# Accumulating DMAs with their addend read from main memory in two halves, and an own program for the first FFN body

## The chip, the cores and the metric

One core of one Trainium2 chip runs the whole kernel. The metric is the device time of one execution in microseconds. TensorE (PE) does the matmuls; ScalarE (ACT), VectorE (DVE) and GpSimd (POOL) prepare operands; SyncE (SP) issues loads. POOL issues the accumulating DMAs. Each engine runs its own instruction list in order, and the lists are tied together by semaphores.

## The reference, cut to what matters

```python
DEPTH, SEQ, D_MODEL = 2, 256, 2048
D_FF = -(-8 * D_MODEL // (3 * 256)) * 256          # 5632
def swiglu(h, w_gate, w_up, w_down):
    return (jax.nn.silu(h @ w_gate) * (h @ w_up)) @ w_down
...
        x = x + rms_norm(m.astype(x.dtype), norm_mix_post[layer])
        h = rms_norm(x, norm_ffn_pre[layer])
        f = swiglu(h, ffn_w_gate[layer], ffn_w_up[layer], ffn_w_down[layer])
        x = x + rms_norm(f.astype(x.dtype), norm_ffn_post[layer])
```

Two layers: the first has a recurrence and a windowed attention as its mixer, the second a differential attention. All is float32. The change touches the FFN (swiglu) of both layers and the last matmuls of the block before it.

## The kernel before, in words

**Split operands.** Every float32 matmul is made of three passes over float32r operands: high part times high part, high times low part of the weight, low part of the activation times high part of the weight. So each 1 MB weight block (128 partitions x 4 x 512) is loaded into a `raw` buffer by SP, ACT copies it to `w_hi` (`hi`, L1035, four buffers), and DVE subtracts to get `w_lo` (`lo`, L1724, three buffers). `lo` of unit u waits until unit u-3 has left PE, `hi` until unit u-4 has.

**The FFN.** The 5632 hidden columns are taken in 11 blocks of 512. The first block is computed in the mixer's style ("head": alternating gate and up units for four row blocks; its last two units are put together by `head_end`, L340). The ten others are computed in ten *bodies*. In body j, PE multiplies the gate and up weights of block j+1 and, beside it, the down projection of block j. Gate and up products are made by a seven-product scheme (P1 to P7, each for the row pairs A and B, 14 units of 12 matmuls); the down projection has four units of 24 matmuls (d0, d1, d3, d2). With eight transposes of the hidden block (`turn`) that makes 18 entries per body. `ENTRIES` gives their order on PE, and the function `block` in each engine's program writes the order out by hand for ACT (L1313), PE (L1669) and DVE (L2079).

**Sums of weights.** P5, P6, P4 and P7 need sums of weight blocks. Four of them (P5A, P6A, P6B, P4B, the `FORMS`) are added in place by DVE (`form`, L1731). The other four (P5B, P7A, P7B, P4A, the `TRANSFERS`) are added in place by an accumulating DMA that POOL issues (`transfer`, L2243): destination `raw[total]`, source `raw[part]`, both on chip, 128 pieces of 8 KB. Before it issues, POOL waits until the total's own `lo` is done and the addend has landed; for P7B also until P5B has landed. ACT's `hi` of that entry waits for the DMA.

**Sums of activations ("lefts").** The scheme also needs sums S1 to S4 of activation blocks for both halves A and B. They are computed once per layer: DVE adds (`left_total`, L1747, 0.7 us each), ACT makes the high part (`left_high`, L1256), DVE the low part (`left_low`, L1787). Before the change S1A, S3A, S2A and S4A are totalled in `head_end`; the low parts of S1A, S2A and S4A too; the rest is made inside the first body, between its entries, under `if body.first`.

**Where the hidden block enters.** `down` (L1637) needs the hidden block transposed: PE's `turn`, ACT's `block_high` (L1251) for `y_hi`, and DVE's `block_low` for `y_lo`. In ACT's `block`, `high(body, "P5A")` stands before `block_high`; in DVE's, `form(P5A)`, `low(d0)`, the four `left_total`s of B (first body only) and `low(P5A)` stand before `block_low`. On PE, d0 follows P1A directly.

**Buffers.** In the FFN eight 1 MB buffers hold weights: three `raw` ones and, by reuse, `gx`, `queries`, `gq` and the two halves of `xs`. `gq` holds the gains of the norm until the block before the head is done (`POST_GAIN`), and `xs` holds the residual, which SP spills to main memory at the end of the head (`spill`). `place_loads` (L580) plans which buffer each load takes, and what it waits for: a buffer is free when the last `lo`, `form` or transfer that reads it is done. `EARLY` loads (d0, g2, u2) are issued ahead of the first body; `released` lists the readers.

Of the kernel before, what the change touches and what calls it, by code (L numbers as in the profile page):

```python
# [27 lines left out]
ALU = mybir.AluOpType  # L28
# [58 lines left out]
class Slot:  # L87


    def __init__(self, u, kg, n, first, last, w, cb=0, region="h", layer=0):  # L90
# [15 lines left out]
FORMS_AHEAD = FORMS[:0]  # L106
# [25 lines left out]
class Body:  # L132


    def __init__(self, layer, j, index, u, e, m, n_head):

        self.layer, self.j, self.index, self.first = layer, j, index, j == 0
        self.base, self.e, self.m = u, e, m
        self.u = {name: u + i for i, name in enumerate(ENTRIES)}
        self.head_gate, self.head_up, self.next, self.prev = n_head, n_head + 1, None, None  # L140
        self.form = {name: len(FORMS) * index + i + 1 for i, name in enumerate(FORMS)}
# [16 lines left out]
def loads_of(body):  # L158

    return tuple(name for name in LOADS if not (body.first and name in EARLY))  # L160

# [20 lines left out]
class Plan:  # L182
# [3 lines left out]
    def __init__(self):  # L186
# [7 lines left out]
        self.place, self.after, self.heads_of, self.head_units, self.x_read, self.wholes, self.last_body = {}, {}, [], [], [], {}, []  # L194

# [144 lines left out]
def head_end(slots, body):  # L340
# [14 lines left out]
    tasks = half(gate, 0) + [Task("early_load", src=body, what=EARLY[2])] + [total(name) for name in TOTALS[:3]]  # L355
    tasks += high_ahead(gate.u - 1, gate) + low_ahead(gate.u - 1, gate) + [left(name) for name in HEAD_LEFT[0]]
    tasks += half(gate, 1) + gate.post + half(up, 0) + [total(TOTALS[3]), Task("spill", 2 * body.layer + 1, slot=up)]
    tasks += high_ahead(gate.u, up) + half(up, 1) + up.post + low_ahead(gate.u, up)
    tasks += [Task("form", src=body, what=name) for name in FORMS_AHEAD] + [left(name) for name in HEAD_LEFT[1]]
# [36 lines left out]
def boundary(b, before, after):  # L396
# [19 lines left out]
    tasks += [hi(u + 11), lo(u + 10), turn(3, 1), lo(u + 11), square(0, 0), hi(u + 12)] + half(a4, 1)  # L416
# [98 lines left out]
def make_plan():  # L515
    plan, before = Plan(), None
    for layer in range(2):
# [14 lines left out]
        plan.head_units.append([slot.u for slot in head])  # L532
        plan.bodies += NF - 1
# [46 lines left out]
def place_loads(plan):  # L580
# [9 lines left out]
    def released(body, name):  # L590
# [7 lines left out]
        def added(entry):  # L598
            if entry in TRANSFERS:
                return entry, 16 * (body.index + 1), body.u[entry] - 1  # L600
            return "form", body.form[entry], body.u[entry] - 1
        if name[0] == "g":
            return (read("P2" + pair), added("P4" + pair)) if second else (read("P4" + pair),)
        return (read("P3" + pair), added("P6" + pair), added("P7" + pair)) if second else (read("P7" + pair),)

    for part in plan.parts:
        for task in part.tasks or ():
            if task.kind == "early_load":
                take((task.src.index, task.what), (RAW + EARLY.index(task.what),), released(task.src, task.what))
            elif task.kind == "tile_unit" or task.kind == "half" and task.t == 0 and task.passes[0] == 0:  # L610
                take(task.slot.u, range(RAW), (("lo", task.slot.u + 1, task.slot.u),))
# [12 lines left out]
def trunk(nc, x, norm_mix_pre, norm_mix_post, norm_ffn_pre, norm_ffn_post,  # L624
# [9 lines left out]
    with ExitStack() as ctx:  # L634
# [198 lines left out]
        def transfer_done(eng, body, name):  # L833

            eng.wait_ge(transferred[name], 16 * (body.index + 1))
# [24 lines left out]
        def _(sp):  # L860
# [5 lines left out]
            def wait_free(waits):  # L866

                for what, value in waits:
# [4 lines left out]
                    elif what in TRANSFERS:  # L873
                        sp.wait_ge(transferred[what], value)
# [79 lines left out]
            def load_slot(slot):  # L954
# [5 lines left out]
                else:  # L960
                    load(slot.u, src)

            def task_of(task):
                if task.kind == "tile_unit" or task.kind == "half" and task.t == 0 and task.passes[0] == 0:
                    load_slot(task.slot)
                elif task.kind == "early_load":
                    if task.what == EARLY[0]:
                        sp.wait_ge(s_done, plan.heads_of[task.src.layer])
                    elif task.what == EARLY[2]:
                        counts = plan.y_counts[2 * task.src.layer + 1]  # L970
                        sp.wait_ge(yg_pool, counts["pool"])
                        sp.wait_ge(yg_dve, counts["dve"])
# [40 lines left out]
        def _(act):  # L1013
# [299 lines left out]
            def block(body):  # L1313
# [8 lines left out]
                if not body.first:  # L1322
                    unload(body.prev, 2, 0)
                seed(body, 0, 1)
                if not body.first:
                    unload(body.prev, 2, 1)
# [6 lines left out]
                if body.first:  # L1333
                    left_high("S1B", body.layer)
# [6 lines left out]
                if body.first:  # L1341
                    left_high("S2B", body.layer)
# [4 lines left out]
                if body.first:  # L1347
                    left_high("S4B", body.layer)
                high(body, "P3B")
                if body.first:  # L1350
                    left_high("S3A", body.layer)
                    left_high("S3B", body.layer)
# [23 lines left out]

            act.dma_start(pre[:, :, :], pre_T).then_inc(pre_in, 16)
# [3 lines left out]
            for part in plan.parts:  # L1381
# [4 lines left out]
                for body in part.bodies:  # L1386
# [8 lines left out]
        def _(pe):  # L1395
# [189 lines left out]
            for part in plan.parts:  # L1585
# [106 lines left out]
                for body in part.bodies:  # L1692
# [6 lines left out]
        def _(dve):  # L1699
# [379 lines left out]
            def block(body):  # L2079
# [4 lines left out]
                if not body.first:  # L2084
                    gated(body.prev, 0)
                if not body.first:
                    gated(body.prev, 1)
                form(body, "P5A")
                low(body, "d0")
                if body.first:  # L2090
                    for name in TOTALS[4:]:
                        left_total(name, body.layer)
# [5 lines left out]
                if body.first:  # L2098
                    left_low("S1B", body.layer)
# [3 lines left out]
                if body.first:  # L2103
                    left_low("S2B", body.layer)
                low(body, "P6B")
                form(body, "P4B")
                if body.first:
                    left_low("S4B", body.layer)
                low(body, "P3B")
                if body.first:  # L2110
                    left_low("S3A", body.layer)
# [196 lines left out]
```

## Time and profile before

| | us |
|---|---|
| median of 3 runs (lowest, highest) | 2176.39 (2174.54, 2178.85) |
| profiled execution, whole | 2174.88 |
| its span, first to last instruction | 2173.1 |
| PE busy | 2145.7 (99%) |
| DVE, ACT, POOL busy | 1700.2, 1490.0, 228.7 |

Each number of a stretch is read from the profiled execution, whose time is 1.5 us under the median. The layers' FFN bodies lie at 423 to 1030 us and at 1525 to 2130 us.

### The profile page before, as it was taken

The numbers are of one execution on the slowest core, as the hardware profiler recorded it, in microseconds if no ns is written. First come the engines' busy times: TensorE is split into PE (matmuls) and PEld (weight loads), VectorE is DVE, ScalarE is ACT, GpSimd is POOL, SyncE is SP. The second block draws the span as 40 slices with busy tenths as digits, with TensorE's granted clock in tenths as the row PEclk, the third lists the DMA queues.
The fourth block names the chain that finished last, engine by engine and source line by source line (L and its number), as shares of the span: only waits on it lengthen the run. The fifth ranks groups of instructions, "written<-read, shape, count | busy, mean of one in ns | idle before, by whom it ended". The sixth has DMA issues, their size and how long they took to land.

```text
span 2173.1 us, 26552 instructions
## 1 busy us (share of the span) xinstructions
PE 2145.7 (99%) x9771; PEld 1767.7 (81%) x9771; DVE 1700.2 (78%) x1538; ACT 1490.0 (69%) x1774; POOL 228.7 (11%) x274
## 2 busy tenths in 40 slices
PE   9999999999999999999999999999999999999998
PEld 7888888778888888888887787788788888888886
DVE  5577467898988888888755656677998888888886
ACT  6677544777777777777655555547677777777774
POOL 0851000000000000000021001001000000000001
PEclk9999999999999999999999999999999999999999
DMA  9545446789999999998564454557899999999984
GB/s 310 190 154 191 155 137 211 242 261 277 264 265 263 302 288 279 282 288 240 177 213 143 150 171 138 187 171 245 244 281 267 303 284 279 284 287 266 266 258 155
DMA packets 226559, 508.82 MB, mean 234 GB/s; under 512 B 13736, under 2 KB 16384, under 8 KB 214656
## 3 DMA queue, kind: packets, MB, share of 16 engines
q1 hardware_dynamic: 214192, 422.68, 55.1%
q0 software_dynamic: 11520, 83.89, 19.5%
q8 instruction: 79, 1.29, 0.2%
q10 hardware_dynamic: 720, 0.56, 0.1%
q14 instruction: 48, 0.39, 0.0%
HBM read 416.92 MB, written 6.29 MB: 195 GB/s over the span
## 4 chain that ended last, share of the span: by engine, by line
PE 93%; DVE 2%; issue 1%; ACT 1%; DMA 1%; SPq 1%; ACTq 0%; POOLq 0%; POOL 0%; DVEq 0%
PE acc L1438 32%; PE acc L1657 20%; PE sc L1451 20%; PE pv L1451 10%; PE acc L1451 5%; PE tp L1465 2%; PE sc L1551 1%; DVE w_lo L1728 1%; PE pv L1580 1%; PE sc L1547 1%; PE pv L1575 1%; DMA raw<-in_ev_w_in 1%; ACT h_hi L1091 0%; PE sc L1530 0%; PE pv L1530 0%
## 5 line engine op out<-in xcount | busy, mean ns | idle before, releaser
L1728 DVE TENSOR_TENSOR w_lo<-raw,w_hi 128x2048 fp32r<-128x2048 f32 x259 | 592.2, 2293 | 103.2 <-PE acc L1438 41.6
L1045 ACT ACTIVATE w_hi<-raw 128x2048 fp32r<-128x2048 f32 x259 | 495.9, 1916 | 135.8 <-PE acc L1438 43.3
L1438 PE MATMUL acc<-w_hi,h_hi 128*128 128x512 f32 x936 | 260.6, 400 | 3.0 <-ACT h_hi L1015 3.0
L1438 PE MATMUL acc<-w_lo,h_hi 128*128 128x512 f32 x936 | 251.8, 391 | 1.0 <-DVE w_lo L1728 0.7
L1438 PE MATMUL acc<-w_hi,h_lo 128*128 128x512 f32 x936 | 251.2, 390 | 0.1
L1728 DVE TENSOR_TENSOR w_lo<-xs,w_hi 128x2048 fp32r<-128x2048 f32 x92 | 210.2, 2288 | 35.9 <-PE acc L1657 20.4
L1438 PEld LDWEIGHTS acc<-w_lo,h_hi 128*128 128x128 f32 x936 | 175.1, 188 | 39.5 <-DVE w_lo L1728 2.3
L1438 PEld LDWEIGHTS acc<-w_hi,h_lo 128*128 128x128 f32 x936 | 175.4, 188 | 37.5 <-DVE h_lo L1703 0.6
L1438 PEld LDWEIGHTS acc<-w_hi,h_hi 128*128 128x128 f32 x936 | 170.6, 188 | 37.2 <-issue 5.8
L1045 ACT ACTIVATE w_hi<-xs 128x2048 fp32r<-128x2048 f32 x92 | 176.1, 1914 | 22.7 <-DVE xs L1741 6.8
L1311 ACT ACTIVATE yacc<-acc 128x512 f32<-128x512 f32 x160 | 95.3, 596 | 132.5 <-PE acc L1657 132.5
L1657 PE MATMUL acc<-w_hi,y_hi 128*128 128x512 f32 x640 | 173.6, 394 | 7.2 <-ACT y_hi L1254 7.2
L1657 PE MATMUL acc<-w_hi,y_lo 128*128 128x512 f32 x640 | 171.5, 390 | 3.4 <-DVE y_lo L1745 3.4
L1657 PE MATMUL acc<-w_lo,y_hi 128*128 128x512 f32 x640 | 173.3, 393 | 0.0
L1657 PEld LDWEIGHTS acc<-w_hi,y_hi 128*128 128x128 f32 x640 | 121.2, 190 | 33.1 <-ACT w_hi L1045 8.0
L1657 PEld LDWEIGHTS acc<-w_hi,y_lo 128*128 128x128 f32 x640 | 120.3, 188 | 29.5 <-DVE y_lo L1745 4.5
L1657 PEld LDWEIGHTS acc<-w_lo,y_hi 128*128 128x128 f32 x640 | 121.9, 190 | 25.6
L1728 DVE TENSOR_TENSOR w_lo<-gx,w_hi 128x2048 fp32r<-128x2048 f32 x52 | 119.0, 2289 | 24.3 <-PE acc L1657 19.4
L1728 DVE TENSOR_TENSOR w_lo<-queries,w_hi 128x2048 fp32r<-128x2048 f32 x52 | 119.0, 2288 | 19.0 <-PE acc L1657 13.4
L1728 DVE TENSOR_TENSOR w_lo<-gq,w_hi 128x2048 fp32r<-128x2048 f32 x46 | 105.3, 2288 | 16.0 <-PE acc L1657 10.2
L1045 ACT ACTIVATE w_hi<-queries 128x2048 fp32r<-128x2048 f32 x52 | 99.7, 1917 | 21.8 <-DVE queries L1741 7.7
L1045 ACT ACTIVATE w_hi<-gx 128x2048 fp32r<-128x2048 f32 x52 | 99.7, 1917 | 18.9 <-DVE gx L1741 6.8
(293 smaller groups left out, 3624.8 us busy)
## 6 DMA issues: line engine op xcount, KB each, us to landing
raw<-in_od_w_in SPq DMA_DIRECT2D x48, 1024.0 KB, 5.1
raw<-in_ffn_w_gate SPq DMA_DIRECT2D x38, 1024.0 KB, 11.2
raw<-in_ffn_w_up SPq DMA_DIRECT2D x38, 1024.0 KB, 9.0
raw<-in_ev_w_in SPq DMA_DIRECT2D x37, 1024.0 KB, 5.4
raw<-in_ffn_w_down SPq DMA_DIRECT2D x36, 1024.0 KB, 7.6
xs<-in_ffn_w_down SPq DMA_DIRECT2D x28, 1024.0 KB, 7.4
xs<-in_ffn_w_up SPq DMA_DIRECT2D x28, 1024.0 KB, 7.6
raw<-xs POOLq DMA_DIRECT2D x18, 1024.0 KB, 13.4
```

Of the source, the lines that this page charges most:

```text
L1045: act.activation(w_hi[u % HI][:, :, :], raw[place.buf][:, :, :], ACT.Copy).then_inc(hi_done, 1)
L1311: act.activation(yacc[:, t, j * KC:(j + 1) * KC], down_banks[k], ACT.Copy).then_inc(drained[k], 1)
L1438: mm = pe.matmul(acc[n % 2][t][:, :], operand(lhs, a, k, t), w[:, k, :], start=first and k == 0 and j == 0, stop=last and k == KT - 1 and ...
L1451: mm = pe.matmul(bank, a[:, k, :], w[:, k, :], start=start and k == 0 and j == 0, stop=stop and k == KT - 1 and j == 2, skip_group_check=c ...
L1465: ins = pe.transpose(dst, src, ident[:, :])
L1547: mm = pe.matmul(sc[:, t, :], q[:, kt, t * P:(t + 1) * P], k[:, kt, task.i % 2, :], start=True, stop=True)
L1551: mm = pe.matmul(sc[:, :, :].rearrange("p m t -> p (m t)"), q[:, kt, t * P:(t + 1) * P], k[:, kt, :, :].rearrange("p m t -> p (m t)"), sta ...
L1575: mm = pe.matmul(pv[:, 0, t * HD:(t + 1) * HD], probT[:, j, t * P:(t + 1) * P], v[:, j, task.i * HD:(task.i + 1) * HD], start=j == 0, stop ...
L1580: mm = pe.matmul(pv[:, 0, 0:CV], flat_pt[:, j * P:(j + 1) * P], v[:, j, hd * CV:(hd + 1) * CV], start=j == 0, stop=j == 1)
L1657: mm = pe.matmul(down_banks[k], a[:, kt, t * P:(t + 1) * P], w[:, kt, :], start=body.first and i == 0 and kt == 0, stop=i == 2 and kt == K ...
L1728: dve.tensor_tensor(w_lo[u % LO][:, :, :], raw[plan.place[u].buf][:, :, :], w_hi[u % HI][:, :, :].bitcast(F32), ALU.subtract).then_inc(lo_ ...
```

## The change

Accumulating DMAs: the addend is read from the weight tensor in main memory, in two DMAs of half the rows each (pieces of 2 KB); the waits for the addend's landing, and of P7B for P5B, are gone; the addend's buffer is no longer held for them. The semaphore is waited for to 32 per body.

In the diff the first `first_block` is ACT's, the second DVE's; PE's follows FIRST_ENTRIES. First body: its own entry order (d3 moved ahead of P6A), own load order, own ACT, PE and DVE lists. d0, g2, u2 and g0 are loaded early. The last up unit of the head is loaded into `gq`, u2 and g0 into `raw` buffers. The totals S1A and S3A move up into `boundary`, the low parts of S2A and S4A down into the body.

```diff
+FIRST_ENTRIES = ("P1B", "P1A", "d0", "P5A", "d1", "P5B", "d3", "P6A", "P6B", "P3B",
+                 "P7A", "P7B", "P3A", "P2A", "P4A", "P2B", "P4B", "d2")
-EARLY = LOADS[:3]
+FIRST_LOADS = ("d0", "g2", "u2", "g0", "u0", "d1", "u1", "u3", "d3", "g1", "g3", "d2")
+EARLY = FIRST_LOADS[:4]
-LEFT = ("S1A", "S2A", "S4A", "S1B", "S2B", "S4B", "S3A", "S3B")
+LEFT = ("S1A", "S1B", "S2A", "S4A", "S2B", "S4B", "S3A", "S3B")
-HEAD_LEFT = (LEFT[:1], LEFT[1:3])
+HEAD_LEFT = LEFT[:1]
...
     gate, up = slots
-    tasks = half(gate, 0) + [Task("early_load", src=body, what=EARLY[2])] + [total(name) for name in TOTALS[:3]]
...
+    tasks = half(gate, 0) + [total(TOTALS[2])]
+    tasks += high_ahead(gate.u - 1, gate) + low_ahead(gate.u - 1, gate) + [left(name) for name in HEAD_LEFT]
+    tasks += half(gate, 1) + gate.post + half(up, 0) + [Task("early_load", src=body, what=name) for name in EARLY[2:]] + [total(TOTALS[3]), Task("spill", 2 * body.layer + 1, slot=up)]
+    tasks += high_ahead(gate.u, up) + half(up, 1) + low_ahead(gate.u, up) + up.post
...
-    tasks += [hi(u + 11), lo(u + 10), turn(3, 1), lo(u + 11), square(0, 0), hi(u + 12)] + half(a4, 1)
+    tasks += [hi(u + 11), lo(u + 10), turn(3, 1), lo(u + 11)]
+    if b % 2:
+        tasks += [Task("left_total", b, b // 2, what=name) for name in TOTALS[:2]]
+    tasks += [square(0, 0), hi(u + 12)] + half(a4, 1)
...
         def added(entry):
-            if entry in TRANSFERS:
-                return entry, 16 * (body.index + 1), body.u[entry] - 1
-            return "form", body.form[entry], body.u[entry] - 1
+            return () if entry in TRANSFERS else (("form", body.form[entry], body.u[entry] - 1),)
...
+            def first_block(body):
+                block_high(body, 0)
+                block_high(body, 1)
+                high(body, "P5A")
+                left_high("S1B", body.layer)
+                high(body, "d1")
+                unload(body, 0, 0)
+                high(body, "P5B")
+                unload(body, 0, 1)
+                copy(body, "P1")
+                left_high("S2A", body.layer)
+                left_high("S4A", body.layer)
+                high(body, "d3")
+                high(body, "P6A")
...
+            def first_block(body):
+                low(body, "d0")
+                block_low(body, 0)
+                form(body, "P5A")
+                block_low(body, 1)
+                left_total("S1B", body.layer)
+                low(body, "P5A")
+                low(body, "d1")
+                left_low("S1B", body.layer)
+                low(body, "P5B")
+                form(body, "P6A")
+                low(body, "d3")
+                form(body, "P6B")
+                left_low("S2A", body.layer)
+                left_low("S4A", body.layer)
+                left_total("S3B", body.layer)
+                left_total("S2B", body.layer)
+                low(body, "P6A")
+                left_total("S4B", body.layer)
+                left_low("S2B", body.layer)
+                low(body, "P6B")
+                left_low("S4B", body.layer)
+                low(body, "P3B")
+                left_low("S3A", body.layer)
+                low(body, "P7A")
+                left_low("S3B", body.layer)
+                low(body, "P7B")
+                low(body, "P3A")
+                low(body, "P2A")
+                form(body, "P4B")
+                low(body, "P4A")
+                low(body, "P2B")
+                low(body, "P4B")
+                upper_part(body, 1)
+                upper_part(body, 0)
+                low(body, "d2")
...
             def transfer(body, name):
...
-                    if "P5" + pair in TRANSFERS:
-                        transfer_done(pool, body, "P5" + pair)
-                    else:
+                    if "P5" + pair not in TRANSFERS:
                         pool.wait_ge(form_done, body.form["P5" + pair])
...
-                pool.wait_ge(landed[part.buf], 16 * part.count)
-                pool.dma_start(raw[total.buf][:, :, :], raw[part.buf][:, :, :], accum_op=ALU.add).then_inc(transferred[name], 16)
+                k = int(addend[1])
+                src = weights["gate" if addend[0] == "g" else "up"][body.layer][k * KC:(k + 1) * KC, (body.j + 1) * KC:(body.j + 2) * KC]
+                for k0 in range(0, KT, KT // 2):
+                    rows = src[k0 * P:(k0 + KT // 2) * P, :].rearrange("(k p) n -> p k n", p=P)
+                    pool.dma_start(raw[total.buf][:, k0:k0 + KT // 2, :], rows, accum_op=ALU.add).then_inc(transferred[name], 16)
```

## Rows read from the trace of the kernel before

**Rows 1.** The page: busy time by engine, and DMA queues with their shares.
```profile
PE 2145.7 (99%) x9771; PEld 1767.7 (81%) x9771; DVE 1700.2 (78%) x1538; ACT 1490.0 (69%) x1774; POOL 228.7 (11%) x274
...
q1 hardware_dynamic: 214192, 422.68, 55.1%
q0 software_dynamic: 11520, 83.89, 19.5%
```

**Rows 2.** Waits of PE over the whole span: total, times, longest.
```profile
PE acc L1657 <- ACT y_hi L1254: 7.2, 2, 3.7
PE acc L1657 <- DVE y_lo L1745: 3.4, 2, 1.8
```

**Rows 3.** PE in order of time: start, length, what; layer 0's first bodies.
```profile
423.23 1.07 PE L1451 MATMUL sc<-w_hi,h_hi 128*128 128x512 f32 x4
...
433.24 2.04 PE L1657 MATMUL acc<-w_hi,y_hi 128*128 128x512 f32 x4 [3.51 <-ACT y_hi L1254]
435.08 1.65 PE L1657 MATMUL acc<-w_lo,y_hi 128*128 128x512 f32 x4
438.50 1.19 PE L1657 MATMUL acc<-w_hi,y_lo 128*128 128x512 f32 x4 [1.77 <-DVE y_lo L1745]
...
443.87 1.08 PE L1451 MATMUL pv<-w_hi,y_hi 128*128 128x512 f32 x4
...
492.84 1.07 PE L1451 MATMUL sc<-w_hi,h_hi 128*128 128x512 f32 x4
...
614.31 1.07 PE L1451 MATMUL sc<-w_hi,h_hi 128*128 128x512 f32 x4
...
661.44 1.07 PE L1451 MATMUL sc<-w_hi,h_hi 128*128 128x512 f32 x4
```

**Rows 4.** PE in order of time: layer 1's first body and the next one's start.
```profile
1525.08 1.07 PE L1451 MATMUL sc<-w_hi,h_hi 128*128 128x512 f32 x4
...
1593.31 1.07 PE L1451 MATMUL sc<-w_hi,h_hi 128*128 128x512 f32 x4
```

**Rows 5.** ACT in order of time, end of the head and layer 0's first body.
```profile
406.68 1.92 ACT L1045 ACTIVATE w_hi<-raw 128x2048 fp32r<-128x2048 f32 x1 [3.77 <-DMA raw<-in_ffn_w_up]
...
430.70 1.91 ACT L1045 ACTIVATE w_hi<-raw 128x2048 fp32r<-128x2048 f32 x1 [5.96 <-DVE raw L1741]
432.51 1.07 ACT L1254 ACTIVATE y_hi<-tp 128x512 fp32r<-128x512 f32 x2
```

**Rows 6.** DVE in order of time, the same stretch.
```profile
428.38 2.28 DVE L1741 TENSOR_TENSOR raw<-raw 128x2048 f32<-128x2048 f32 x1
430.58 2.28 DVE L1728 TENSOR_TENSOR w_lo<-gx,w_hi 128x2048 fp32r<-128x2048 f32 x1
432.78 0.68 DVE L1778 TENSOR_TENSOR yacc<-yacc 128x512 f32<-128x512 f32 x1
...
435.56 2.28 DVE L1728 TENSOR_TENSOR w_lo<-raw,w_hi 128x2048 fp32r<-128x2048 f32 x1
437.76 1.28 DVE L1745 TENSOR_TENSOR y_lo<-tp,y_hi 128x512 fp32r<-128x512 f32 x2
```

**Rows 7.** Busy time of each engine in one later body (stretch, PE, PEld, DVE, ACT, POOL, clock, DMA share, GB/s).
```profile
614.30:675.00 60.70, 60.70 (x273) 50.39 (x272) 53.12 (x29) 47.05 (x42) 3.44 (x4) 1.00 0.92 277
```

**Rows 8.** One accumulating DMA of that body: POOL's issue, ACT's and DVE's use; landing times.
```profile
609.07 0.87 POOL L2257 DMA_DIRECT2D gx<-raw  x1 [35.42 <-DVE w_lo L1728]
...
621.34 1.91 ACT L1045 ACTIVATE w_hi<-gx 128x2048 fp32r<-128x2048 f32 x1
...
626.35 2.29 DVE L1728 TENSOR_TENSOR w_lo<-gx,w_hi 128x2048 fp32r<-128x2048 f32 x1 [0.95 <-PE acc L1657]
...
gx<-raw POOLq DMA_DIRECT2D x1, 1024.0 KB, 8.9
```

**Rows 9.** DMA rate of the stretch 604 to 672 us in 40 slices.
```profile
GB/s 387 387 388 388 328 211 212 116 226 222 104 289 312 235 236 245 414 117 207 169 231 10 0 25 298 399 401 393 389 387 388 386 386 386 387 387 383 388 386 401
```

More of the change, by code:

```diff
@@ L158, in loads_of @@
 def loads_of(body):
-    return tuple(name for name in LOADS if not (body.first and name in EARLY))
+    return FIRST_LOADS[len(EARLY):] if body.first else LOADS
 class Part:
@@ L1320, in high_next @@
                         hi(u)
-                if not body.first:
-                    unload(body.prev, 2, 0)
+                unload(body.prev, 2, 0)
                 seed(body, 0, 1)
-                if not body.first:
-                    unload(body.prev, 2, 1)
+                unload(body.prev, 2, 1)
                 high(body, "P5A")
@@ L1385, in _ @@
                     continue
-                for body in part.bodies:
+                first_block(part.bodies[0])
+                for body in part.bodies[1:]:
                     block(body)
@@ L1690, in block @@
                     down(body, 2)
-                for body in part.bodies:
+                def first_block(body):
+                    quarter_product(body, "P1B")
+                    turn(body, 0)
+                    turn(body, 1)
+                    quarter_product(body, "P1A")
+                    down(body, 0)
+                    quarter_product(body, "P5A")
+                    down(body, 1)
+                    quarter_product(body, "P5B")
+                    down(body, 3)
+                    quarter_product(body, "P6A")
+                    quarter_product(body, "P6B")
+                    quarter_product(body, "P3B")
+                    quarter_product(body, "P7A")
+                    quarter_product(body, "P7B")
+                    quarter_product(body, "P3A")
+                    quarter_product(body, "P2A")
+                    quarter_product(body, "P4A")
+                    quarter_product(body, "P2B")
+                    quarter_product(body, "P4B")
+                    down(body, 2)
+                first_block(part.bodies[0])
+                for body in part.bodies[1:]:
                     block(body)
@@ L2082, in low_next @@
                     lo(body.base + len(ENTRIES) + ENTRIES.index(name))
[L2084 to L2087, printed above, removed]
+                gated(body.prev, 0)
+                gated(body.prev, 1)
                 form(body, "P5A")
                 low(body, "d0")
-                if body.first:
-                    for name in TOTALS[4:]:
-                        left_total(name, body.layer)
                 low(body, "P5A")
@@ L2102, in block @@
                 low(body, "P6A")
-                if body.first:
-                    left_low("S2B", body.layer)
                 low(body, "P6B")
                 form(body, "P4B")
-                if body.first:
-                    left_low("S4B", body.layer)
                 low(body, "P3B")
-                if body.first:
-                    left_low("S3A", body.layer)
-                    left_low("S3B", body.layer)
                 low(body, "P7A")
@@ L2125, in block, with first_block @@
                 low_next("P1A")
+            def first_block(body):
+                low(body, "d0")
[33 more added lines that the diff above has]
+                low(body, "d2")
+                low(body.next, "P1B")
+                low(body.next, "P1A")
             for section in plan.parts:
@@ L2131, in _ @@
                     continue
-                for body in section.bodies:
+                first_block(section.bodies[0])
+                for body in section.bodies[1:]:
                     block(body)
```

74 lines of the change are left out of this document (42 added, 32 removed).

## The prediction, made before the change was run

> **What bounds the kernel now.** First the page [rows 1]: PE is busy 2145.7 of 2173.1 us, so whatever the change does elsewhere, it can take away only time in which PE stands or runs slowly. Next the waits of PE [rows 2]: almost all of its waiting is in one line, the down projection (L1657), two times for `y_hi` (7.2 us together) and two times for `y_lo` (3.4 us), that is once in each layer. The order of time [rows 3] shows where: in the first body. P1B begins at 423.23, d0 should follow P1A at about 429.6, but begins at 433.24, and P5A, which follows d0, begins at 443.87. The length of a body is read from the starts of P1B: the first body takes 492.84 - 423.23 = 69.61 us, the next two 614.31 - 492.84 = 121.47, so 60.73 each. The first body of layer 0 thus loses 8.88 us. Layer 1 [rows 4]: 1593.31 - 1525.08 = 68.23, a loss of 7.50. Together **16.4 us**, more than the 10.6 us of waits, because the granted clock also falls to half in parts of this stretch: four matmuls that take 1.07 us elsewhere take 2.04 and 1.65 [rows 3]. The eighteen later bodies lose nothing: in one of them PE is busy 60.70 of 60.70 us [rows 7].
>
> **Why d0 waits.** ACT does nothing for 5.96 us and then `hi(P5A)` at 430.70, because DVE's sum for P5A is done only at 430.6; `y_hi` stands behind it in ACT's list and begins at 432.51 [rows 5], though PE had made its transposes before P1A. `y_lo` stands on DVE behind the sum (428.38), `lo(d0)` (430.58), four totals (from 432.78) and `lo(P5A)` (435.56), and begins at 437.76 [rows 6].
>
> **Part 1, the first body's own lists.** ACT does both `y_hi` before `hi(P5A)`: they no longer wait for DVE. The transposes end at about 426.7 (P1B's 2.7 us and eight transposes after 423.23), so `y_hi` is ready at about 427.7, before d0 can start at 429.5. On DVE `lo(d0)` comes first, and `y_lo` for the first half at once behind it. The full 16.4 us of loss goes if nothing else is late. What is late next is DVE, for its work moves, it does not vanish:
> - One step of `lo` or of a sum is 2.20 us (430.58 to 432.78, and 428.38 to 430.58 [rows 6]), a small operation 0.6 to 0.7.
> - DVE can start `lo(d0)` at about 424.1: its unit waits for the last up unit (423.2) and for the two gated products of the hidden block. For that DVE must be earlier in the head than now. It is: the last up unit's load moves from a `raw` buffer to `gq`, which was free ten microseconds earlier, and the 3.77 us for which ACT waits for that load [rows 5] go; and S1A and S3A move into time in which DVE idles.
> - Until `lo(P4A)` is done DVE has 13 `lo`s and 4 sums, 17 x 2.20 = 37.4 us, and 2 `y_lo`, 4 totals and 7 low parts, 13 x 0.63 = 8.2 us; it waits some 0.9 us for `y_hi` and 1.35 us for `hi(P5A)`, which can begin only when the sum is done. 424.1 + 47.9 = 472.0.
> - PE wants it in P4A's second pass. Without a loss P4A begins 661.44 - 614.31 = 47.1 us into a body [rows 3] (d3's place ahead of it does not matter), at 470.4, and its second pass 0.9 later, at 471.3.
>
> So PE loses about 0.7 us there; the entries before it have margins of 0 to 1.5 us. The second body then starts with DVE less ahead than now, and its `y_lo` may be 0.2 to 0.3 us late. I take **1.0 us of new loss for each layer**. Bounds: nothing (the small operations overlap), or 3 us (DVE reaches `lo(d0)` 1.5 us later, as it would without the gain in the head, and each of some ten handovers between ACT and DVE costs 0.05 more).
>
> The moved loads: SP issues u0, d1, u1 and u3 in place of g0, u1, u0, d1, u3, and d1 holds the queue until `lo` of the last up unit's neighbour is done (about 411 to 413). All of these are wanted after 428; d3 is issued after `lo(d0)` (426) and wanted at 445. I cost this at nothing. Cover: 15 us or more between landing and use.
>
> **Part 2, the DMAs.** In the later bodies PE never waits, so earlier free buffers and the dropped waits bring **nothing**; they can only cost. What they cost is DMA time. From the page [rows 1]: ordinary loads take 0.551 x 2173.1 = 1197 us of all 16 engines for 422.68 MB, 2.97 us for 1.05 MB (89 ns for each of 214192 packets). The 80 accumulates take 0.195 x 2173.1 = 424 us, 5.30 us each. One body has 12 loads and 4 accumulates: 35.6 + 21.2 = 56.8 of 60.7 us; the DMA share of one body, 0.92 [rows 7], agrees. After the change an accumulate is 512 pieces of 2 KB, not 128 of 8 KB. No row shows such a piece. By its bytes alone: 5.30 us again, 166 ns a piece. If it costs two ordinary 2 KB packets (one for the source, one for the destination): 179 ns, 5.7 us, and the body's DMA work is 58.5 us, still under 60.7. If it costs three, 268 ns, 8.6 us. I take 179 ns, for the accumulate of now also costs about two ordinary transfers of its bytes (5.30 against 2 x 2.97). The bound for hiding is (60.7 - 35.6)/4 = 6.3 us, **196 ns a piece**.
>
> Landing: P5B's accumulate is issued at 609.07, lands in 8.9 us, and ACT uses its total at 621.34, 12.3 us after the issue; DVE uses it at 626.35, and only after a wait for PE [rows 8]. The second half adds one issue of POOL (0.87 us; up to twice that for more pieces) and, with 2 KB pieces taking turns with 2 KB loads, some 2 us. That is 12 to 13 us against 12.3, with some 3 us more before DVE's `lo` would be late. So nothing at PE. POOL's issues grow from 4 to 8 a body, 3.5 us to some 10, on an idle engine.
>
> **Sum.** 16.4 - 2 x 1.0 = 14.4 us. The profiled execution would go from 2174.88 to 2160.5; the median stands 1.5 us above it, so **2162**. Its own range is 2158 (no new loss) to 2166 (3 us in each layer).
>
> **The rivals.**
> - *DMA becomes the bound* (slower). Place: the 18 later bodies. Price at 268 ns a piece: 35.6 + 34.3 = 69.9 us for a body, 9.2 more, x 18 = 165, less 14.4: about 2327. It decides from 202 ns a piece, where a body is 0.8 us longer (14.4/18) and the gain is used up. For it: the loads already run at 386 to 401 GB/s in long stretches [rows 9], with little idle between them. Against it: 128 pieces of 8 KB cost just their bytes twice. Milder forms, one late landing a body, give 2180 to 2200. Chance 0.14.
> - *The source in main memory makes an accumulate some 1.2 times as dear*: 5.30 x 1.22 = 6.5 us, four of them 25.9, a body 61.5, so +0.8 x 18 = 14: the gain is gone, 2176. Against it: ordinary loads read main memory at 387 to 401 GB/s [rows 9], and the change raises what a body reads only to 16 x 1.05 MB in 60.7 us, 276 GB/s. Chance 0.06. The Trainium skill, SBUF: State Buffer, "Summary: rules for kernel authors", speaks for this rival: one should reckon about 358 GB/s where main memory is an end of the transfer and 436 only from SBUF to SBUF, a ratio of 1.22 (by that rule, as an estimate, 2176). The trace disagrees on the first figure, since rows 9 stand above it.
> - *The loss moves inside the first body*: DVE or ACT is late for several entries instead of one, 3 to 5 us in each layer. DVE's work there is some 54 us of 60.7, against 53.1 in a later body [rows 7] that has no such late start. Gain 16.4 - 2 x 4 = 8: 2168. Chance 0.14.
> - *More than the sum*: DVE isn't late at all and small gaps in the head also go: 2155 to 2158. Chance 0.05.
>
> **How the numbers follow.** The forecast (2158 to 2166) has 0.61. The range reaches over the moved loss and up to the case without gain, 2156 to 2174; the slow rival and most of the last two tenths stay out. A difference of 0.2% (4.4 us) is about what a measurement of this kernel can tell from no change. Faster than 2172.0: 0.61 + 0.14 + 0.05 = 0.80, less 0.01 for a moved loss that takes all; within: 0.07; slower: 0.14.
>
> **What would show it.** In the changed trace: PE's waits for `y_hi` and `y_lo` in L1657 gone; d0 starts near 6.3 us after P1B and the granted clock stays full; the first bodies are 61 to 63 us, the later ones 60.7; if PE waits in the first body, it is for `w_lo`, around P4A; ACT does not wait for the load of the last up unit. Packets of the software queue rise to some 43,000, and its share stays near 20%. Wrong if a later body is over 60.9 us, if that share is above 24% (0.195 x 6.3/5.3 is 23%), or if ACT waits for accumulates in many bodies.

## The result and the profile after

The changed kernel takes **2468.89 us** (median of 4 runs, 2460.05 to 2477.22) against 2175.47 (4 runs, 2174.22 to 2178.85): ratio 1.1345, 95% interval 1.1303 to 1.1387. It is 293 us slower, where 14 us faster was forecast. The profiled run took 2467.82 us, its span is 2466.0.

The page, as in [rows 1] (busy time by engine; queues with packets, MB, share of 16 DMA engines' span):
```profile
PE 2196.6 (89%) x9771; PEld 1793.6 (73%) x9771; DVE 1693.3 (69%) x1538; ACT 1469.4 (60%) x1774; POOL 361.8 (15%) x354
...
q1 hardware_dynamic: 214192, 422.68, 50.0%
q0 software_dynamic: 43520, 83.90, 20.8%
```
The DMA engines are not the bound: both queues' packets together take 70.8% of their time, less than the 74.6% of before. PE now stands still for 2466.0 - 2196.6 = 269 us, and is busy 51 us longer with the same instructions. Its waits, as in [rows 2] (total us, times, longest):
```profile
PE sc L1486 <- ACT probT L1287: 232.9, 20, 12.9
PE sc L1486 <- DVE w_lo L1787: 11.2, 13, 1.8
PE sc L1486 <- ACT rgx L1287: 7.5, 2, 4.0
```
The waits for `y_hi` and `y_lo` of [rows 2] are gone. A new one, for `probT`, stands once in each of the 20 bodies, 9 to 13 us long. PE in order of time, as in [rows 3] (start, length, what, wait before):
```profile
423.09 1.07 PE L1486 MATMUL sc<-w_hi,h_hi 128*128 128x512 f32 x4
...
429.42 1.07 PE L1692 MATMUL acc<-w_hi,y_hi 128*128 128x512 f32 x4
...
653.28 1.07 PE L1486 MATMUL sc<-w_hi,h_hi 128*128 128x512 f32 x4
...
695.29 2.08 PE L1486 MATMUL sc<-w_hi,lefts 128*128 128x512 f32 x4 [11.04 <-ACT probT L1287]
697.16 1.91 PE L1486 MATMUL sc<-w_lo,lefts 128*128 128x512 f32 x4
...
728.10 1.07 PE L1486 MATMUL sc<-w_hi,h_hi 128*128 128x512 f32 x4
```
In the first body d0 begins 6.33 us after P1B and does not wait, as forecast. But the body as a whole takes 81.1 us (the next P1B begins at 504.21), not 61 to 63, with a wait of 11.05 us for `probT` in it. A later body takes 728.10 - 653.28 = 74.8 us, not 60.7. In its middle PE stands for 11.04 us, and then four matmuls take 1.91 and 2.08 us instead of 1.07: from 695.3 to 700.5 the granted clock is 0.50 of full, the lower level of 1.2 GHz. The same stands behind the wait in the other bodies, and it accounts for the 51 us of extra busy time. The same body by engine (columns as in [rows 7]):
```profile
653.28:728.10 74.82, 63.78 (x274) 52.26 (x272) 52.30 (x29) 45.94 (x42) 9.73 (x8) 0.91 0.81 223
```
The DMA share fell from 0.92 to 0.81. PE waits for `probT`, a small step of ACT. What holds ACT is in its order of time, same body:
```profile
665.03 1.92 ACT L1047 ACTIVATE w_hi<-gq 128x2048 fp32r<-128x2048 f32 x1 [4.64 <-DMA gq<-in_ffn_w_up]
...
677.85 1.92 ACT L1047 ACTIVATE w_hi<-raw 128x2048 fp32r<-128x2048 f32 x1 [0.98 <-DMA raw<-in_ffn_w_up]
...
692.84 1.91 ACT L1047 ACTIVATE w_hi<-xs 128x2048 fp32r<-128x2048 f32 x1 [12.09 <-DMA xs<-in_ffn_w_up]
694.66 0.58 ACT L1287 ACTIVATE probT<-sc 128x512 f32<-128x512 f32 x1
```
These three `w_hi` are P5B, P7A and P7B, the totals that the accumulating DMAs make. `hi(P7B)` stands 12.09 us for its total, with `probT` behind it. And POOL, which issues those DMAs (`gq` is P5B, `raw` P7A, `xs` P7B, `gx` P4A; as in [rows 8]). Ahead of P7A and P7B the program waits for the load of the total's own block, and ahead of P7A for DVE's sum P5A as well; ahead of P5B and P4A it waits for `lo`:
```profile
649.15 1.21 POOL L2343 DMA_DIRECT2D gq<-in_ffn_w_up  x1 [23.07 <-DVE w_lo L1787]
657.85 1.22 POOL L2343 DMA_DIRECT2D gq<-in_ffn_w_up  x1 [7.49 <-issue]
665.28 1.21 POOL L2343 DMA_DIRECT2D raw<-in_ffn_w_up  x1 [6.20 <-issue]
671.45 1.22 POOL L2343 DMA_DIRECT2D raw<-in_ffn_w_up  x1 [4.96 <-issue]
678.10 1.21 POOL L2343 DMA_DIRECT2D xs<-in_ffn_w_up  x1 [5.43 <-issue]
684.47 1.22 POOL L2343 DMA_DIRECT2D xs<-in_ffn_w_up  x1 [5.15 <-issue]
693.09 1.21 POOL L2343 DMA_DIRECT2D gx<-in_ffn_w_gate  x1 [7.40 <-issue]
```
This is the view that decides. The program puts **no wait** between the two halves of a total, yet the second is issued 6 to 9 us after the first, and the idle time is labelled "issue": the engine waited for nothing that the profile knows. The spacing is about the time in which such a half lands (median 6.0 to 8.0 us in the list of DMA issues). So six halves run one after the other from 649.15 until the total of P7B can be read at 692.84: 43.7 us.

A *descriptor* is the entry that tells a DMA engine one piece to move. **Theory A, room for descriptors.** POOL writes the descriptors of such a DMA into an on-chip scratch of fixed size, the constant SCRATCH, 1024 bytes in both kernels. A half of 256 pieces takes more than half of it, so the next one can be issued only when the one before has landed. **Theory B, the pieces**: 2 KB pieces are slow, whatever the room. **Theory C, main memory**: reading the addend there is slow. **Theory D**: the first body's new program does the harm.

### The profile page after: what moved, and what is told of

It reads as the page before. It is cut to its first block, busy times and chain, and to the rows that moved or that the text cites. A ratio compares the mean times of both kernels' runs of the same rounds, so it can differ in the third digit from the quotient of the medians.

```text
span 2466.0 us, 26555 instructions
## 1 busy us (share of the span) xinstructions
PE 2196.6 (89%) x9771; PEld 1793.6 (73%) x9771; DVE 1693.3 (69%) x1538; ACT 1469.4 (60%) x1774; POOL 361.8 (15%) x354
## 3 DMA queue, kind: packets, MB, share of 16 engines
q0 software_dynamic: 43520, 83.90, 20.8%
## 4 chain that ended last, share of the span: by engine, by line
PE 40%; issue 37%; DMA 8%; POOL 6%; DVE 6%; ACT 2%; SPq 0%; ACTq 0%; DVEq 0%; POOLq 0%
PE acc L1473 30%; DVE w_lo L1787 5%; POOL raw L2343 3%; PE sc L1486 3%; DMA raw<-in_ffn_w_gate 2%; DMA xs<-in_ffn_w_up 2%; PE tp L1500 2%; POOL xs L2343 1%; DMA xs<-in_ffn_w_gate 1%; PE sc L1586 1%; PE acc L1486 1%; PE acc L1692 1%; DMA queries<-in_ffn_w_gate 1%; DMA gq<-in_ffn_w_gate 1%; POOL queries L2343 1%
## 5 line engine op out<-in xcount | busy, mean ns | idle before, releaser
L1787 DVE TENSOR_TENSOR w_lo<-raw,w_hi 128x2048 fp32r<-128x2048 f32 x269 | 615.8, 2294 | 225.9 <-ACT w_hi L1047 164.6
L1047 ACT ACTIVATE w_hi<-raw 128x2048 fp32r<-128x2048 f32 x269 | 513.9, 1914 | 319.7 <-DMA raw<-in_ffn_w_up 162.7
L1486 PE MATMUL sc<-w_hi,lefts 128*128 128x512 f32 x320 | 113.6, 488 | 232.9 <-ACT probT L1287 232.9
L1787 DVE TENSOR_TENSOR w_lo<-xs,w_hi 128x2048 fp32r<-128x2048 f32 x76 | 173.5, 2288 | 142.3 <-ACT w_hi L1047 131.5
L1486 PEld LDWEIGHTS sc<-w_hi,lefts 128*128 128x128 f32 x320 | 75.5, 243 | 257.8 <-ACT probT L1287 241.3
L1047 ACT ACTIVATE w_hi<-xs 128x2048 fp32r<-128x2048 f32 x76 | 145.2, 1911 | 172.6 <-DMA xs<-in_ffn_w_up 134.5
L1047 ACT ACTIVATE w_hi<-gq 128x2048 fp32r<-128x2048 f32 x54 | 103.3, 1914 | 58.0 <-DMA gq<-in_ffn_w_gate 25.7
L1787 DVE TENSOR_TENSOR w_lo<-gq,w_hi 128x2048 fp32r<-128x2048 f32 x54 | 123.5, 2287 | 13.3 <-ACT w_hi L1047 7.6
L2343 POOL DMA_DIRECT2D raw<-in_ffn_w_up x52 | 63.3, 1217 | 456.2 <-issue 266.4
```

What stands on the lines that cost most here:

```text
L1047: act.activation(w_hi[u % HI][:, :, :], raw[place.buf][:, :, :], ACT.Copy).then_inc(hi_done, 1)
L1486: mm = pe.matmul(bank, a[:, k, :], w[:, k, :], start=start and k == 0 and j == 0, stop=stop and k == KT - 1 and j == 2, skip_group_check=c ...
L1787: dve.tensor_tensor(w_lo[u % LO][:, :, :], raw[plan.place[u].buf][:, :, :], w_hi[u % HI][:, :, :].bitcast(F32), ALU.subtract).then_inc(lo_ ...
L2343: pool.dma_start(raw[total.buf][:, k0:k0 + KT // 2, :], rows, accum_op=ALU.add).then_inc(transferred[name], 16)
```

## The experiments

Ratios are against the kernel before on the same chip (medians 2176.45, 2175.95 or 2176.16 us), with a 95% interval; where no interval stands there was one run.

**1. Which part: the first body alone, the DMAs alone.** `e2_first_body` is the changed kernel with the accumulates, waits and releases of before:
```diff
-                for k0 in range(0, KT, KT // 2):
-                    rows = src[k0 * P:(k0 + KT // 2) * P, :].rearrange("(k p) n -> p k n", p=P)
-                    pool.dma_start(raw[total.buf][:, k0:k0 + KT // 2, :], rows, accum_op=ALU.add).then_inc(transferred[name], 16)
+                pool.wait_ge(landed[part.buf], 16 * part.count)
+                pool.dma_start(raw[total.buf][:, :, :], raw[part.buf][:, :, :], accum_op=ALU.add).then_inc(transferred[name], 16)
```


> The changed kernel with the accumulating DMAs put back as they were before: one DMA, addend from the buffer on chip, pieces of 8 KB, with its waits for the addend. The first body's program and load order stay new. Theories 1 and 2: the first bodies take 61 to 62 us and the later ones 60.7, so 14 to 16 us less than the kernel before, 2159 to 2163 us. Theory 3: stays slow, over 2400 us.

`e3_new_dma` is the kernel before with the opposite edit.

> The kernel before with only the accumulating DMAs changed: addend from main memory, two halves, waits and buffer releases as in the change; the first body as before. Theories 1 and 2: the slowness is all here, 2480 to 2490 us (the change's 2469 and the first bodies' 16 us). Theory 3: about 2176 us.

Measured: e2 **2159.49** (5 runs, 2158.3 to 2160.01), ratio 0.9922 [0.991, 0.9935]; e3 **2468.07** (1 run). Waits of PE in e3:
```profile
PE sc L1447 <- ACT probT L1281: 219.9, 20, 13.2
PE acc L1653 <- ACT y_hi L1250: 7.3, 2, 3.7
```
The new DMAs alone make the whole loss, and leave the old wait for `y_hi` where it was. D falls; with the old DMAs the first body's program is worth 17.0 us. With the new ones it is worth nothing: e3 was expected at 2480 to 2490, 16 us above the changed kernel, and came out level with it, a miss. The first body shows why. PE in e3:
```profile
466.71 1.20 PE L1447 MATMUL sc<-w_hi,lefts 128*128 128x512 f32 x4 [0.87 <-ACT probT L1281]
```
There PE waits only 0.87 us for `probT`, where the changed kernel waits 11.05: PE's old stand for `y_hi` and `y_lo` hides most of the wait for the accumulates. The two losses overlap and do not add up. e3's first body takes 76.9 us, the changed kernel's 81.1.

**2. The size of the scratch.** Only the constant changes:
```diff
-SCRATCH = 1024
+SCRATCH = 1216
```


> Only edit to the changed kernel: the scratch region for the descriptors of the accumulating DMAs is 1216 bytes a partition, not 1024. Theory 1 (room for descriptors): with 1024 bytes only one half of an accumulate fits, so GpSimd issues the next half when the one before has landed, 6 to 8 us apart; with 1216 two fit. Then in P7A, P7B the issues stand in pairs, PE's wait of 11 us a body before P7B goes, a body takes 60.7 to 64 us and the kernel 2160 to 2220 us. Theory 2 (pieces of 2 KB or main memory as source are dear in themselves): the room changes nothing, about 2469 us and issues 6 to 8 us apart. Theory 3 (the first body's program or the buffer plan): about 2469 us too.

> The changed kernel with 1088 bytes of scratch, 64 more than the change has. If a 256-piece half takes two 16-byte entries a piece and one for its end on each of 16 engines, that is 33 entries, 528 bytes: two halves want 1056 bytes, so 1024 holds one and 1088 holds two, and the time is that of the run with 1216, about 2180 us. If a half takes more room than 544 bytes, one half at a time: about 2469 us.

Measured: `e1_ring1216` **2179.99** (10 runs, 2174.53 to 2184.87), ratio 1.0013 [1.0003, 1.0023]; `e8_ring1088` **2178.03** (1 run). POOL in e1:
```profile
604.89 2.46 POOL L2343 DMA_DIRECT2D gq<-in_ffn_w_up  x2 [27.71 <-DVE w_lo L1787]
617.16 2.47 POOL L2343 DMA_DIRECT2D raw<-in_ffn_w_up  x2 [9.81 <-issue]
629.56 2.48 POOL L2343 DMA_DIRECT2D xs<-in_ffn_w_up  x2 [9.93 <-issue]
638.45 2.45 POOL L2343 DMA_DIRECT2D gx<-in_ffn_w_gate  x2 [6.42 <-issue]
```
64 bytes more take away 291 us, with every DMA, piece and source as before. A is shown; B and C cannot be the cause of the 290 us. The halves now go in pairs ("x2"), and the next pair still waits, by the spacing until the last has landed, 9 to 12 us apart. The row below is of a stretch of nine later bodies in e1 (columns as in [rows 7]); PE still loses 7 us in it:
```profile
484.00:1030.00 546.00, 538.88 (x2396) 443.99 (x2396) 465.37 (x249) 405.73 (x371) 86.99 (x71) 1.00 0.95 266
```

**3. More room.** For 2048 bytes space had to be made: `junk`, a tile whose content nobody reads, shares the space of others.
```diff
-SCRATCH = 1024
+SCRATCH = 2048
-        junk = sb("junk", [P, KC], BF16)
+        junk = lqk.bitcast(BF16)
+        first_junk = stage[:, 0, 0:KC // 2].bitcast(BF16)
...
```


> The changed kernel with 2048 bytes of scratch (for which the square's throwaway output is put into buffers that are idle then). Three halves of an accumulate can be on the way. The run with 1216 bytes left 20 us against the run with the first body's program alone. If those are still round trips of pairs of halves, they go: 2158 to 2166 us, PE never waits for an accumulate. If they are the price of 2 KB pieces on DMA engines that are 95% busy, they stay: 2174 to 2185 us and the DMA share stays at 0.95.

Measured: **2160.58** (5 runs, 2159.03 to 2161.73), ratio 0.9927 [0.9914, 0.9941]. POOL in one body, and the same nine bodies by engine:
```profile
599.55 2.45 POOL L2344 DMA_DIRECT2D gq<-in_ffn_w_up  x2 [32.93 <-DVE w_lo L1788]
606.04 1.20 POOL L2344 DMA_DIRECT2D raw<-in_ffn_w_up  x1 [4.05 <-DVE gx L1801]
608.56 1.22 POOL L2344 DMA_DIRECT2D raw<-in_ffn_w_up  x1 [1.31 <-issue]
609.29 1.74 POOL L2344 DMA_DIRECT2D xs<-in_ffn_w_up  x1
617.64 1.20 POOL L2344 DMA_DIRECT2D xs<-in_ffn_w_up  x1 [6.61 <-issue]
```
```profile
484.00:1030.00 546.00, 546.00 (x2447) 452.82 (x2447) 478.21 (x253) 421.52 (x376) 85.30 (x70) 1.00 0.97 271
```
PE is busy for all 546 us, although the DMA engines are busy 0.97 of the time. The change as such works and reaches 2160.6, forecast 2162, as soon as there is room. (Where `junk` lies was not tried by itself; e10 below has it moved too, and there the waits are back.) This also settles what was left in e1: the waiting of the pairs, not the load on the DMA engines. It gives the deadline too. Here ACT takes the total of P7B (`w_hi<-xs`) at 630.56, without a wait for the DMA, 31.0 us after P5B's issue at 599.55. In the changed kernel six halves in a row needed 43.7 us, 12.7 too many; ACT waited 12.09 us there and PE 11.04. In e1 three pairs needed 33.3 us, 2.3 too many, by ACT's row of the same body:
```profile
638.14 1.92 ACT L1047 ACTIVATE w_hi<-xs 128x2048 fp32r<-128x2048 f32 x1 [2.30 <-DMA xs<-in_ffn_w_up]
```
So little did not reach PE: this body took 60.7 us. From P5B's issue to P4A's e1 takes 29 to 37 us in its 20 bodies, and PE waits for `probT` in seven of them, 4.1 us at most.

**4. How much room a DMA takes.** `e4_quarters`: four DMAs of 128 pieces of 2 KB for each total, scratch 1024.
```diff
-                for k0 in range(0, KT, KT // 2):
-                    rows = src[k0 * P:(k0 + KT // 2) * P, :].rearrange("(k p) n -> p k n", p=P)
+                for k0 in range(KT):
+                    rows = src[k0 * P:(k0 + 1) * P, :].rearrange("(k p) n -> p k n", p=P)
...
```


> The changed kernel with each accumulate in four DMAs of 128 pieces of 2 KB, not two of 256; scratch stays 1024 bytes. Theory 1: a quarter needs half the descriptors of a half, so three are on the way at once; the chain of single round trips of 6 to 8 us is gone or much shorter, 2160 to 2300 us. If GpSimd can have only one DMA on the way whatever its size: twice as many round trips, over 2700 us. Theory 2 (2 KB pieces from main memory): same bytes and pieces as the change, about 2469 us or more.

Measured: **2318.64** (1 run). POOL:
```profile
556.89 2.68 POOL L2343 DMA_DIRECT2D raw<-in_ffn_w_up  x3 [22.41 <-DVE w_lo L1787]
565.74 0.86 POOL L2343 DMA_DIRECT2D raw<-in_ffn_w_up  x1 [6.17 <-issue]
```
Three go at once, the fourth waits 6.17 us: the count of three came as expected, the time did not. It was put at 2160 to 2300 us and came out 19 above that. Stalls are left between the quarters, and PE waits for `probT` in all 20 bodies, 100.3 us together. `e10_whole2048` is e7 with one DMA of 512 pieces for each total:
```diff
-                for k0 in range(0, KT, KT // 2):
-                    rows = src[k0 * P:(k0 + KT // 2) * P, :].rearrange("(k p) n -> p k n", p=P)
+                rows = src.rearrange("(k p) n -> p k n", p=P)
...
```


> The changed kernel with 2048 bytes of scratch, and each accumulate as one DMA of 512 pieces of 2 KB. By the count of entries it takes 65 of 128, so one at a time, but only four round trips of some 10 to 12 us a body in place of eight. P7B's issue waits for P7A's landing, as in the change. Theory 1: later bodies of 61 to 68 us, 2165 to 2300 us, and issues never closer than 9 us. If the count is wrong and two fit: about 2160 us with P7A and P7B issued within 4 us.

Measured: **2172.56** (1 run): 12 us above e7. POOL:
```profile
602.19 1.29 POOL L2343 DMA_DIRECT2D gq<-in_ffn_w_up  x1 [26.21 <-DVE w_lo L1788]
612.99 1.30 POOL L2343 DMA_DIRECT2D raw<-in_ffn_w_up  x1 [9.51 <-issue]
622.72 1.29 POOL L2343 DMA_DIRECT2D xs<-in_ffn_w_up  x1 [8.43 <-issue]
```
One at a time even in 2048 bytes, but there are only three up to P7B's total: 632.37 (the next issue) less 602.19 is 30.2 us here, just about the 31.0 there are. In the 20 bodies it is 29 to 37, and PE waits for `probT` in seven of them (8.1 us together). `e11_before512` takes room away from the kernel before:
```diff
-SCRATCH = 1024
+SCRATCH = 512
```


> The kernel before with 512 bytes of scratch, not 1024. A whole accumulate of 128 pieces of 8 KB takes 17 entries of 32 by the count, so now one is on the way at a time. P7B was issued 3 us after P7A; it will wait for P7A's landing, some 6 to 8 us later, but it was used 21 us after its issue: so no loss, 2174 to 2180 us. If any wait for room is costly, over 2200 us.

Measured: **2176.10** (10 runs, 2174.39 to 2178.69), ratio 0.9999 [0.999, 1.0008]. POOL:
```profile
609.32 0.87 POOL L2257 DMA_DIRECT2D gx<-raw  x1 [33.53 <-DVE w_lo L1728]
618.61 0.88 POOL L2257 DMA_DIRECT2D raw<-xs  x1 [8.42 <-DMA gx<-raw]
627.75 0.87 POOL L2257 DMA_DIRECT2D raw<-xs  x1 [8.26 <-issue]
```
P7B is issued at 627.75 instead of 618.55: the same stall in the kernel before, and nothing lost: the total has landed by P4A's issue at 635.34, and ACT takes it only at 640.24. A stall is therefore not enough for a loss; the row of stalls must be longer than the slack.

A count that fits every run: a DMA takes for each of the 16 DMA engines two entries of 16 bytes for each of its pieces there, and one at the end. 128 pieces: 17 entries, 272 bytes; three fit into 1024 and not four (e4), one into 512 and not two (e11). 256 pieces: 33 entries, 528 bytes; one fits into 1024 and two into 1088. 512 pieces: 65 entries, 1040 bytes; one fits into 2048 and not two. The rule is worked out from these thresholds; no row shows an entry. They leave some play: two entries at the end instead of one would fit every run too, and so would none, if the room may never be quite full. For one at the end speak the packets on the pages: each accumulate DMA has 16 more of them than pieces (43,520 / 160 = 272 for 256, 11,520 / 80 = 144 for 128), one for each DMA engine.

**5. The source, and the size of the pieces.** Both are e2 (addend on chip, scratch 1024) with each accumulate in two halves: `e5_onchip_4k` along the row (128 pieces of 4 KB a half), `e6_onchip_2k` with every other 2 KB row (256 pieces a half).
```diff
-                pool.dma_start(raw[total.buf][:, :, :], raw[part.buf][:, :, :], accum_op=ALU.add).then_inc(transferred[name], 16)
+                for k0 in range(0, KT, KT // 2):
+                    pool.dma_start(raw[total.buf][:, k0:k0 + KT // 2, :], raw[part.buf][:, k0:k0 + KT // 2, :], accum_op=ALU.add).then_inc(transferred[name], 16)
```
e6, in place of those two lines:
```diff
+                for k0 in range(2):
+                    pool.dma_start(raw[total.buf][:, k0::2, :], raw[part.buf][:, k0::2, :], accum_op=ALU.add).then_inc(transferred[name], 16)
```


> First body's program as changed; accumulates in two halves, but the addend from the buffer on chip, so 128 pieces of 4 KB a half; scratch 1024; the old waits for the addend. Theory 1 (room for descriptors): a half takes 17 entries of 64, three are on the way, about 2160 us, as with whole accumulates. If it is the cutting in two that costs (each half pays its own round trip): over 2300 us.

> As the run with 4 KB pieces, but each half takes every other 2 KB of a partition's row, so 256 pieces of 2 KB, still from the buffer on chip; scratch 1024. Theory 1: the room holds one half, issues 6 to 8 us apart, 2440 to 2490 us though main memory isn't read. If main memory as source is what makes the change slow: about 2160 to 2180 us.

Measured: e5 **2158.82**, e6 **2423.84** (1 run each). POOL in e5, then in e6:
```profile
600.12 1.75 POOL L2348 DMA_DIRECT2D gq<-gx  x2 [33.47 <-DVE w_lo L1791]
```
```profile
651.86 1.22 POOL L2348 DMA_DIRECT2D gq<-gx  x1 [5.63 <-DVE xs L1804]
658.19 1.21 POOL L2348 DMA_DIRECT2D raw<-xs  x1 [5.11 <-issue]
665.52 1.22 POOL L2348 DMA_DIRECT2D raw<-xs  x1 [6.12 <-issue]
```
Two halves for a total cost nothing while each has 128 pieces. With 256 pieces the loss is there again with the addend on chip, so C falls as the cause. e6 missed its expectation by 16 us on the low side: its loss over e5 is 265 us, that of the changed kernel over e2 309. In the rest of 44 us the source may have a part: from the first issue to the seventh, six halves take 39.8 us on average in e6 and 45.1 in the changed kernel (19 bodies each). But the old waits and releases differ too, and the two were not tried apart.

**6. Does the gain of the first body need its whole program?** `e9_reorder` is the kernel before, with both `y_hi` ahead of `hi(P5A)` on ACT and the first steps of DVE's list in the order below, in the first body alone; the head, the entries, the loads and the low parts stay (DVE's part):
```diff
-                form(body, "P5A")
-                low(body, "d0")
                 if body.first:
+                    low(body, "d0")
+                    block_low(body, 0)
+                    form(body, "P5A")
+                    block_low(body, 1)
                     for name in TOTALS[4:]:
                         left_total(name, body.layer)
-                low(body, "P5A")
-                block_low(body, 0)
-                block_low(body, 1)
+                    low(body, "P5A")
+                else:
...
```


> The kernel before, with only two things of the first body moved: ACT makes both y_hi ahead of hi(P5A), and DVE makes lo(d0), then y_lo for the first half, the sum for P5A, y_lo for the second half, the four totals and lo(P5A). Head, loads, entry order and low parts stay. If the loss in the first body was the place of these two steps alone, nearly all of the 16.4 us goes: 2160 to 2163 us. If the moved head work, load order and the new entry order are needed as well, DVE is late by some 2 to 4 us a layer and the time is 2164 to 2168 us.

Measured: **2172.68** (11 runs, 2171.54 to 2175.15), ratio 0.9986 [0.9976, 0.9995]: a miss. PE:
```profile
429.09 1.07 PE L1661 MATMUL acc<-w_hi,y_hi 128*128 128x512 f32 x4
...
438.77 1.19 PE L1455 MATMUL pv<-w_lo,y_hi 128*128 128x512 f32 x4 [2.37 <-DVE w_lo L1732]
...
441.08 1.91 PE L1661 MATMUL acc<-w_hi,y_hi 128*128 128x512 f32 x4
```
d0 no longer waits, but P5A waits 2.37 us for its low part, which stands behind four totals, and the granted clock falls again (1.91 us). 3.5 us are left of 17.0. So what e9 leaves out (the totals and low parts moved, the entry order, the head, the loads) carries most of the gain. Which one of them was not tried.

## Why the prediction was wrong

**Part 1 was right in its mechanism, and nearly in size.** Forecast: 14.4 us, 2174.88 to 2160.5 in the profiled execution. e2's profiled run, without Part 2, took 2160.01, 14.9 less; the medians give 17.0, 2.6 more than forecast. (The forecast calls 2158 the case of no new loss; by its own terms that case is 2176.4 - 16.4 = 2160.0, and e2's median lies just below it.) PE in e2:
```profile
423.79 1.07 PE L1490 MATMUL sc<-w_hi,h_hi 128*128 128x512 f32 x4
...
430.13 1.07 PE L1696 MATMUL acc<-w_hi,y_hi 128*128 128x512 f32 x4
...
470.93 1.07 PE L1490 MATMUL sc<-w_hi,h_hi 128*128 128x512 f32 x4
472.11 1.21 PE L1490 MATMUL sc<-w_lo,h_hi 128*128 128x512 f32 x4
...
484.98 1.07 PE L1490 MATMUL sc<-w_hi,h_hi 128*128 128x512 f32 x4
```
The first body takes 484.98 - 423.79 = 61.19 us, a new loss of 0.46 and not 1.0; layer 1's takes 61.19 too. It lies partly where the sum put it, in P4A's second pass (472.11, not 471.8). No wait of PE in e2 is one for a moved load.

**Part 2, what the DMAs cost: the sum held, with a term too small.** Packets 43,520, forecast some 43,000. Share of the software queue 20.8%. An accumulate takes, by e7's page (22.9% of 2158.8 us over 80), 6.18 us, where 5.7 were taken; the bound for hiding was 6.3. It was nearer than forecast, and e7 shows that it held: DMA share 0.97, no loss in the later bodies.

**The step that failed is the landing of Part 2**: "The second half adds one issue of POOL (0.87 us; up to twice that for more pieces)", and with it "on an idle engine". The cost of issuing was nearly right (1.21 us), but it was counted as if POOL could always issue. The missing term is the room: the second half cannot be issued until the first has landed, and so on through the queue. The slack was taken as 12.3 us for one total, when what counts is the row of six halves up to P7B, wanted 31.0 us after the first issue (in the kernel before too: ACT takes it at 640.04, the first issue is at 609.07 [rows 8]). At the 7.3 us found (43.7/6) six are 12.7 too many for ACT. At PE it was 11.04 us in this body and 232.9 in all 20, with shorter waits and the lower clock behind on top.

The prediction named three signs of being wrong, and two came: ACT waits for accumulates in many bodies, and a later body takes 74.8 us, over 60.9. The third did not: the queue's share is 20.8%, under 24%, and that sets the mechanism apart from the rivals. Of the forecast signs, d0's start and the packets came in the changed kernel; a full clock and first bodies of 61 to 63 us came only without the stalls, in e2 (61.2) and e7 (61.1, and 62.8 in layer 1).
- *DMA becomes the bound* has the right sign and the wrong mechanism: the DMA share fell to 0.81. Its milder form, "one late landing a body, 2180 to 2200", is the shape of what came, priced at less than a tenth of its size.
- *The source in main memory* falls as a cost in time: e2 and e7 differ by 1.1 us. An accumulate of 2 KB pieces takes 6.41 us of the DMA engines from main memory (20.8% of 2466.0 over 80) and 6.06 from the chip (e6, 20.0% of 2422.1), a ratio of 1.06. The Trainium skill, SBUF — State Buffer, "Summary: rules for kernel authors", whose ratio of 1.22 spoke for it, is not borne out here.
- *The loss moves inside the first body*: no, by e2, though e9 shows that it does with half of the reordering.

Where the 293 us are: against e7, which differs in room and in where `junk` lies, the changed kernel's span is 307.2 us longer. PE idles 269.4 instead of 2158.8 - 2141.7 = 17.1, which is 252.3, and is busy 2196.6 - 2141.7 = 54.9 longer at the lower clock. Less the gain of e7's profiled run over the one of before, 2173.1 - 2158.8 = 14.3, these are the 293.

**The best version** is any of three: e2 (2159.49), e7 (2160.58) and e5 (2158.82, one run). Reading the addend from main memory brings nothing in time over reading it on chip.

## What to carry to other kernels

Before a software-issued DMA is cut into more pieces, count its descriptors against the scratch that they are written into, and count how many such DMAs must be under way at once: the cost is not in the bytes or in the issue, but in one DMA waiting for another to land. In a profile the sign is a DMA issue with idle time labelled "issue" of about a landing's length in front of it, with no wait in the program. The label alone is not enough, as P7B in the kernel before shows:
```profile
618.55 0.86 POOL L2257 DMA_DIRECT2D raw<-xs  x1 [2.14 <-issue]
```
There the program does wait, for P5B to land (609.07 and 8.9 us). A stall like that costs nothing until the row of them up to the first use is longer than the slack, so add the whole row, not one of its members.

## What was not expected of the hardware

- The room is a cliff: 1024 bytes 2468.9 us, 1088 bytes 2178.0, 2048 bytes 2160.6, and the kernel before does with 512.
- An accumulating DMA seems to take two entries a piece and not one: with one, a half of 256 pieces would take 17 entries and three would fit into 1024 bytes, but only one did. Whether a plain DMA of POOL takes fewer, no run here shows. The Trainium skill, DMA: Bandwidth & Descriptors, "The descriptor swizzle", gives for a plain 1 MB transfer 9 read descriptors an engine, 8 of them data. The Trainium skill, Collectives: The Full Stack, "The bandwidth ceiling: the fold count and why AG ≠ RS ≠ AR", says of collectives that a reduce emits two read descriptors a chunk; the thresholds here agree with two.
- POOL's issue takes 0.87 us for 128 pieces, 1.21 for 256 and 1.30 for 512, by the rows above: little beside the stall.
- Each wait of 9 to 13 us cost PE another 2.7 us on average (54.9 us over 20 bodies) after its end, since the matmuls behind it run at the lower clock (0.50 of full in the body shown).
